# Second block's entry in three fp32r products with halves made on three engines, and 4 MB gate/up transfers for experts 18 to 29

## The reference, cut to what matters

```python
h = rmsnorm(x, g_attn_norm)
proj = h @ w_in                     # [256, 1024] @ [1024, 928]: 512 columns u, 256 q_lat, 128 kv_lat, 32 k_r
y_pool = pool_mixer(u, w_pool, b_pool, pool_scale)
y_attn = mla_attention(q_lat, kv_lat, k_r, cos, sin, g_q_a, w_q_b, g_kv_a, w_kv_b)
mix = concatenate([rmsnorm(y_pool, g_out_pool), rmsnorm(y_attn, g_out_attn)])
x = x + mix @ w_out
x = x + moe(rmsnorm(x, g_ffn_norm), ...)   # 32 experts, top 4 per token
return rmsnorm(x, g_final)
```

## Time and profile before

| | us |
|---|---|
| median of 3 runs | 1413.59 |
| range of the runs | 1408.78 to 1415.08 |
| profiled execution, its own time | 1410.57 |
| span of that execution | 1408.8 |

### The profile page before, as it was taken

The page is one execution under the profiler, slowest core; times in us unless marked ns, Lnnn a source line. Parts: engine busy times, 40 slices in busy tenths (PEclk is TensorE's granted clock), DMA queues, the critical chain, the costliest instruction groups (busy, mean ns, idle before and its releaser), DMA issues.

```text
span 1408.8 us, 21679 instructions
## 1 busy us (share of the span) xinstructions
PE 1360.4 (97%) x7688; PEld 775.7 (55%) x7689; DVE 755.0 (54%) x1157; ACT 304.4 (22%) x461; POOL 725.6 (52%) x727
## 2 busy tenths in 40 slices
PE   8999999999999999999999999999989999999997
PEld 7899989999967744334334334334333343334332
DVE  7575788887675545445356535444354453433322
ACT  5645453334325201001001001001000010001001
POOL 3000023332154078888878988888888888500000
PEclk9999999999999999999999999999999999999999
DMA  9444355555448899999999999999999999999996
GB/s 322 156 147 148 120 180 180 179 179 179 170 178 287 342 378 429 428 428 428 427 408 425 428 428 428 428 428 428 428 428 427 429 428 428 428 428 428 428 424 266
DMA packets 78283, 480.81 MB, mean 341 GB/s; under 512 B 7115, under 2 KB 31368, under 8 KB 53160
## 3 DMA queue, kind: packets, MB, share of 16 engines
q1 hardware_dynamic: 74910, 477.71, 83.5%
q10 hardware_dynamic: 3338, 2.62, 0.6%
HBM read 479.26 MB, written 1.05 MB: 341 GB/s over the span
## 4 chain that ended last, share of the span: by engine, by line
PE 55%; DMA 22%; issue 15%; POOL 5%; DVE 2%; ACT 0%; POOLq 0%; SPq 0%; DVEq 0%; ACTq 0%
DMA stage<-in_w_gate_up 14%; PE bank L2480 13%; DMA stage<-in_w_down 8%; PE bank L2158 7%; PE bank L1928 6%; PE bank L2588 6%; PE bank L2186 4%; POOL ring_b L677 3%; POOL ring L677 2%; PE bank L1878 2%; PE bank L2085 2%; PE bank L2123 2%; PE bank L1944 2%; PE bank L2466 1%; PE bank L2530 1%
## 5 line engine op out<-in xcount | busy, mean ns | idle before, releaser
L2480 PE MATMUL bank<-ring,x_T 128*64 128x512 f32 x1552 | 349.2, 596 | 22.1 <-POOL ring L677 16.2
L677 POOL COPY ring_b<-stage 128x1024 f32<-128x1024 f32 x252 | 264.9, 1097 | 47.1 <-DMA stage<-in_w_down 23.5
L2480 PEld LDWEIGHTS bank<-ring,x_T 128*64 128x64 f32 x1552 | 106.4, 137 | 244.1 <-issue 195.3
L2588 PE MATMUL bank<-ring_b,act_T 128*64 128x512 f32 x1056 | 233.9, 595 | 0.5 <-ACT act_T L1022 0.5
L677 POOL COPY ring<-stage 128x1024 f32<-128x1024 f32 x192 | 198.2, 1078 | 35.3 <-DMA stage<-in_w_gate_up 26.7
L1735 DVE TENSOR_TENSOR h<-h,bank 128x512 f32<-128x512 f32 x124 | 79.7, 684 | 190.8 <-PE bank L2530 190.8
L2588 PEld LDWEIGHTS bank<-ring_b,act_T 128*64 128x64 f32 x1056 | 72.9, 137 | 144.3 <-issue 129.4
L1711 DVE SCALAR_TENSOR_TENSOR y_lo<-bank,slot_gate,y_hi 128x512 fp32r<-128x512 f32 x33 | 24.8, 751 | 207.4 <-ACT y_hi L1002 207.4
L533 POOL TENSOR_TENSOR rstd<-msq,neg_half 128x2 f32<-128x2 f32 (+2 forms) x9 | 7.7, 856 | 240.7 <-DVE msq L1089 221.2
L574 POOL TENSOR_TENSOR ff_lo<-ring,ff_hi 128x2048 fp32r<-128x2048 f32 x11 | 53.0, 4818 | 145.2 <-PE bank L2158 96.6
L1016 ACT ACTIVATE sig<-bias_raw 128x512 f32<-128x512 f32 x33 | 20.8, 629 | 489.4 <-DVE bias_raw L1746 489.4
(11 more groups left out here) (491 smaller groups left out, 2124.4 us busy)
## 6 DMA issues: line engine op xcount, KB each, us to landing
stage<-in_w_gate_up SPq DMA_DIRECT2D x73, 2048.0 KB, 15.1
stage<-in_w_down SPq DMA_DIRECT2D x38, 2048.0 KB, 15.2
stage_b<-in_w_gate_up SPq DMA_DIRECT2D x25, 2048.0 KB, 15.0
ring<-in_w_gate_up SPq DMA_DIRECT2D x21, 2048.0 KB, 23.8
ring_b<-in_w_down SPq DMA_DIRECT2D x13, 2048.0 KB, 23.0
stage_b<-in_w_down SPq DMA_DIRECT2D x12, 2048.0 KB, 15.2
ring<-in_w_in SPq DMA_DIRECT2D x22, 1024.0 KB, 5.2
ring<-in_w_ffn_in SPq DMA_DIRECT2D x22, 1024.0 KB, 6.2
```

The lines of the kernel that those rows point to most:

```text
L677: ins = pool.tensor_copy(pair_slot(g, k)[:, cols], stage_place(g, place)[:, cols])
L2480: ins = pe.matmul(banks[n][rows, :], t.x_T[:, c, :], job_slot(g, c)[:, c0:c0 + 512], start=False, stop=(c == GU - 1), skip_group_check=True)
L2588: ins = pe.matmul(banks[4][rows, :], t.act_T[:, k, SLOTS * (c // 2):SLOTS * (c // 2) + SLOTS], job_slot(g, GU + c)[:, c0:c0 + 512], start= ...
```

## The change

1. *Entry in three products.* ACT rounds the four chunks of w_in_2 (`entry_rounded`, order 0, 3, 1, 2; high parts in free places of `ff_hi` and in a new `w_u_hi`) and the four quarters of the normalised rows (`rows_rounded`). The rests are spread: DVE chunk 0, half of chunk 3 and half of chunk 2, POOL chunk 1 and the other halves (`entry_rest`), and POOL the four quarters of `h_n_lo`. SP issues chunk 3 ahead of chunk 2. PE's `lat0`, `lat1`, `u1`, `u0` take three fp32r products each in a new order.
2. *Squares.* The squares of `x_n` go from DVE to ACT (`gained_square`).
3. *Constants.* POOL's constants for the routing move from the start of the entry to behind the pooling windows.
4. *Gate/up in quads.* `STAGED = E - 14`: experts 2 to 17 are staged. For experts 18 to 29 SP loads gate/up as two transfers of 4 MB (`load_quad`, rows of 32 KB), each when TensorE has used both pairs; POOL waits for each quad and passes it on to the two pairs' semaphores. Expert 30 is loaded in parts of 2 MB, expert 31 in halves as before. So that a quad is contiguous in SBUF, pairs 0 and 1 lie in `ring`, pairs 2 and 3 in `ring_b`; SP's early loads of parts 2 and 3 of expert 0 are swapped with it.
5. *Row order.* A partition now holds four neighbouring rows of w_gate_up, so ACT writes `h_n` permuted and the gathers read 128 contiguous columns.

The diff, cut to its core:

```diff
-STAGED = E - 6
+STAGED = E - 14
+STAGED_USES = 16 * (PLACES + (STAGED - 2) * PARTS) // PLACES
...
+ENTRY = 4
+ENTRY_ORDER = (0, 3, 1, 2)
+def entry_made(c):
+    return ENTRY_ORDER.index(c) + 1
...
 # sync_program
+    def load_quad(e, quad):
+        sp.dma_start(quad_slot(g, quad), gate_up[e, quad]).then_inc(s.staged[0] if quad else s.quad_in, 16)
...
-    for n, (src, shape, _) in enumerate(g.second):
+    for n in (0, 1, 3, 2, *range(4, len(g.second))):
+        src, shape, _ = g.second[n]
...
-    with sp.Fori(STAGED - 1, E - 2) as m:
+    with sp.Fori(STAGED - 1, E - 3) as m:
         last = last_job(m)
-        for k in range(PARTS):
+        for quad in range(2):
+            sp.wait_ge(*part_used(g, last, 2 * quad + 1))
+            load_quad(m + 1, quad)
+        for k in range(PAIRS, PARTS):
             next_part(m + 1, last, k)
...
 # gpsimd_program
+    def entry_rest(c, half=None):
+        slot, cols = slot_use(g.n_second + c)[0], entry_cols(c, half)
+        pool.wait_ge(s.pa_rounded, entry_made(c))
+        pool.tensor_tensor(t.ring_r[:, slot, cols], t.ring[:, slot, cols], entry_high(g, c)[:, cols].bitcast(F32),
+                           ALU.subtract).then_inc(s.pa_split, 1)
+    entry_rest(1)
+    entry_rest(3, 1)
+    for n, (b, h) in enumerate((b, h) for b in range(NB) for h in range(2)):
+        rows, toks = slice(4 * h, 4 * h + 4), slice(b * P, b * P + P)
+        pool.wait_ge(s.h_rounded, 2 * NB + n + 1)
+        pool.tensor_tensor(t.h_n_lo[:, rows, toks], t.h_nT2[:, rows, toks], t.h_n_hi[:, rows, toks].bitcast(F32),
+                           ALU.subtract).then_inc(s.h_split_pool, 1)
     pool.wait_ge(s.ff_o, FF_STEPS)
...
     pool.tensor_tensor(mean, mean, r1, ALU.mult).then_inc(s.rstd_ready, 1)
+    entry_rest(2, 1)
     rsqrt("lat")
...
 # scalar_program
+    entry_rounded(0)
+    act.wait_ge(s.ff_g, FF_STEPS)
+    act.wait_ge(s.ff_o, FF_STEPS - 1)
+    for c in ENTRY_ORDER[1:]:
+        entry_rounded(c)
+    square("end1", s.rows_added, 2, 0, scratch)
+    rows_rounded(0, 0)
+    rows_rounded(0, 1)
+    act.wait_ge(s.act_msq, squares + 1)
+    square("end1", s.rows_added, 4, 1, scratch)
+    rows_rounded(1, 0)
+    act.wait_ge(s.act_msq, squares + 2)
+    gained_square(0)
+    rows_rounded(1, 1)
+    act.wait_ge(s.act_msq, squares + 3)
+    gained_square(1)
...
 # vector_program
+    entry_rest(0)
+    entry_rest(3, 0)
     dve.wait_ge(s.gains, 1)
     for b, n in ((0, 0), (0, 1), (1, 0)):
         add_rows(b, n)
     for h in range(2):
         turned_rows(0, h)
     add_rows(1, 1)
-    for h in range(2):
-        turned_rows(1, h)
+    turned_rows(1, 0)
     dve.wait_ge(s.small_in, 16 * 5)
-        dve.tensor_tensor(t.x_n[:, b, :], t.h[:, b, :], t.g_rows[:], ALU.mult).then_inc(s.h_gained, 1)
+    gained(0)
+    turned_rows(1, 1)
+    gained(1)
+    entry_rest(2, 0)
+    dve.wait_ge(s.act_msq, ACT_SQUARES["end1"])
...
 # tensor_program
+    LATENT = ((t.h_n_hi, wl_hi), (t.h_n_hi, wl_lo), (t.h_n_lo, wl_hi))
+            if k % 4 == 0 and part == 0:
+                pe.wait_ge(s.h_rounded, 2 * NB + 2 * b + k // 4 + 1)
+                pe.wait_ge(s.pa_rounded, entry_made(k // 4))
+            if k % 4 == 0 and part == 1:
+                pe.wait_ge(*((s.pa_split, 1) if k else (s.w_split, SPLIT + 1)))
+            if k % 4 == 0 and part == 2:
+                pe.wait_ge(s.h_split_pool, 2 + 2 * b + k // 4 + 1)
+    first = open_bank(r2, "lat0")
+    latents(first, 0, 0)
+    pe.wait_ge(s.rows_added, 2 * NB)
+    turn_quarter(r2, "nT", t.h, 1, 1)
+    latents(first, 0, 1)
+    other = open_bank(r2, "lat1")
+    for k0 in (0, 4):
+        for part in range(2):
+            latents(other, 1, part, k0, k0 + 4)
+    latents(first, 0, 2).then_inc(s.filled, 1)
+    latents(other, 1, 2).then_inc(s.filled, 1)
...
-            k_rows = slice(2 * P * (f // 2) + f % 2, 2 * P * (f // 2) + 2 * P, 2)
+            k_rows = slice(P * f, P * f + P)
```

More of the change, by code:

```diff
@@ L255, in build @@
         t.persistent(into(ctx))
[L257 removed]
+        for phase in (t.vectors, t.mixer, t.branches, t.ffn, t.attention, t.entry, t.last_out, t.experts):
             with ExitStack() as stack:
@@ L688, in gpsimd_program @@
                 put_in_place(last, k, place, m * 48 + 16 * landed)
+    with pool.Fori(0, E - 2 - STAGED) as m:
+        for quad in range(2):
+            pool.wait_ge(*((s.staged[0], m * 16 + (STAGED_USES + 16)) if quad else (s.quad_in, m * 16 + 16)))
+            pool.sem_inc(s.turn_begun, 1)
+            for pair in (2 * quad, 2 * quad + 1):
+                pool.sem_inc(s.in_place[pair], 16)
     rsqrt("end2")
@@ L913, in scalar_program, with entry_rounded, rows_rounded, gained_square @@
     act.preload_act_table_set("natural_log_exp_and_others")
-    for b in range(NB):
-        square("end1", s.rows_added, 2 * b + 2, b, t.y_att[:].rearrange("p b n -> p (b n)"))
-        if b == 0:
-            act.wait_ge(s.act_msq, ACT_SQUARES["end1"] - 1)
+    def entry_rounded(c):
+        slot, value = slot_use(g.n_second + c)
+        act.wait_ge(s.landed[slot], value)
+        act.activation(entry_high(g, c)[:, entry_cols(c)], t.ring[:, slot, entry_cols(c)],
+                       ACT.Copy).then_inc(s.pa_rounded, 1)
+    def rows_rounded(b, h):
+        rows, toks = slice(4 * h, 4 * h + 4), slice(b * P, b * P + P)
+        act.wait_ge(*r2.drained(f"nT{b}{h}"))
+        act.activation(t.h_n_hi[:, rows, toks], t.h_nT2[:, rows, toks], ACT.Copy).then_inc(s.h_rounded, 1)
+    def gained_square(b):
+        act.wait_ge(s.h_gained, b + 1)
+        act.activation(scratch, t.x_n[:, b, :], ACT.Square,
+                       accum_out=t.msq[:, NORM_AT["end1"], NB + b:NB + b + 1]).then_inc(s.act_msq, 1)
+    scratch = t.y_attn[:].rearrange("p b n -> p (b n)")
+    squares = ACT_SQUARES["end1"] - 2 * NB
+    entry_rounded(0)
[14 more added lines that the diff above has]
+    gained_square(1)
     act.wait_ge(s.rstd_ready, NORM_AT["attn"] + 1)
@@ L1442, in turned_rows, with entry_rest, gained @@
                           spread(t.gain2[:, 4 * h:4 * h + 4], P), ALU.mult).then_inc(done, 1)
+    def entry_rest(c, half=None):
+        slot, cols = slot_use(g.n_second + c)[0], entry_cols(c, half)
+        dve.wait_ge(s.pa_rounded, entry_made(c))
+        dve.tensor_tensor(t.ring_r[:, slot, cols], t.ring[:, slot, cols], entry_high(g, c)[:, cols].bitcast(F32),
+                          ALU.subtract).then_inc(s.w_split, 1)
+    def gained(b):
+        dve.wait_ge(s.rows_added, 2 * b + 2)
+        dve.tensor_tensor(t.x_n[:, b, :], t.h[:, b, :], t.g_rows[:], ALU.mult).then_inc(s.h_gained, 1)
+    k = NORM_AT["end1"]
+    entry_rest(0)
+    entry_rest(3, 0)
     dve.wait_ge(s.gains, 1)
@@ L2235, in tensor_program, with entry_parts, entry_weights @@
-    landed(n + 2)
-    landed(n + 3)
-    wu = halves(n + 2, 512)
-    def u_block(bank, i, j, k0=0, k1=KT):
+    def entry_parts(c):
+        slot, cols = slot_use(n + c)[0], entry_cols(c)
+        return [w[:, cols].rearrange("p (k m) -> p k m", k=4) for w in (entry_high(g, c), t.ring_r[:, slot, :])]
+    def entry_weights(c0):
+        parts = [entry_parts(c) for c in (c0, c0 + 1)]
+        return [[parts[k // 4][i][:, k % 4, :] for k in range(KT)] for i in range(2)]
+    wl_hi, wl_lo = entry_weights(0)
@@ new lines, in tensor_program, with latents @@
+    LATENT = ((t.h_n_hi, wl_hi), (t.h_n_hi, wl_lo), (t.h_n_lo, wl_hi))
+    def latents(bank, b, part, k0=0, k1=KT):
+        x, wt = LATENT[part]
+        for k in range(k0, k1):
+            if k % 4 == 0 and part == 0:
[5 more added lines that the diff above has]
+                pe.wait_ge(s.h_split_pool, 2 + 2 * b + k // 4 + 1)
+            ins = pe.matmul(bank[:, 0:416], x[:, k, b * P:(b + 1) * P], wt[k][:, 0:416],
+                            start=(part == 0 and k == 0), stop=(part == 2 and k == KT - 1))
+        return ins
@@ L2245, in u_block @@
         return ins
     into = open_bank(r2, "u1")
-    u_block(into, 1, 0)
+    for part in range(2):
+        u_block(into, 1, 0, part)
     pe.wait_ge(s.diag_ready, NB)
@@ L2253, in tensor_program @@
     ins.then_inc(s.filled, 1)
-    u_block(into, 1, 1, 0, 6)
+    for part in range(2):
+        u_block(into, 1, 1, part)
+    u_block(into, 1, 0, 2)
+    u_block(into, 1, 1, 2, 0, 4)
     pe.wait_ge(s.lat_ready, 2 * NB)
@@ L2278, in tensor_program @@
     into = open_bank(r2, "u0")
-    u_block(into, 0, 0)
-    u_block(into, 0, 1).then_inc(s.filled, 1)
+    for j in range(2):
+        for part in range(3):
+            ins = u_block(into, 0, j, part)
+    ins.then_inc(s.filled, 1)
     def bias(m, o):
```

127 lines of the change are left out of this document (71 added, 56 removed).

## The result

The changed kernel takes 1417.89 us (median of 8 executions, 1416.34 to 1424.68), the kernel before 1410.2 in executions taken beside it (8, 1408.78 to 1415.08). The ratio is 1.0056, with a 95% interval of 1.0041 to 1.0072: slower by 7.7 us. The profiled execution took 1416.46 us, its span is 1414.5 against 1408.8.

A forecast was written before the change was run, and what follows sets the result against it. The last 900 us were taken as bound by expert weight transfers, whose start hangs on TensorE's entry. Entry +7.4, gathers -0.6 and -1.2, transfers -2.4 sum to +3.2 us: 1416.8 for the median, range 1408 to 1422.5.

The forecast's parts named there:

- Products of the entry: Entry on TensorE: three fp32r products per step save 4.2 us if all halves are ready, bounds 3.5 and 4.9.
- Chunk 3 and DVE: Entry: DVE waits for chunk 3, first add_rows at 394.0, TensorE stands from 389.7 to 394.9, latents start at 398.2.
- DVE and POOL hold each other up: Entry: SBUF work of both engines stands in one line, 10.9 us, making rsqrt("end1") 7.5 us late, at 409.2.
- Behind it: Entry after rsqrt("end1"): latents' transposes start 8.9 us late, heads' transposes 7.4 us late.
- Constants: POOL's constants moved behind the pooling cost nothing; without idle time to cover them, up to 6 us.
- Gathers: Contiguous gather columns: -0.6 us ahead of the stream, -1.2 us at the expert with two jobs.
- Transfers: Gate/up of experts 18 to 29 in 32 KB rows: -2.4 us from fewer packets, bounds 0 and -4.8.
- The rival from the Trainium skill: Transfers: 2 MB already gives full bandwidth, so 32 KB packets bring nothing; 1419.2 us, chance 10%.
- Direct loading: From expert 18 on: zero cost, up to +1 us; TensorE's 4.9 us later start is caught up within the job.
- the second: Rival: clock falls to half in TensorE's entry gap if over about 4 us; 1419.8 to 1422.2 us, chance 20%.
- DVE and POOL don't queue: Rival on the entry: the engines alternate with little loss; entry +2 to +3, total 1412 us, chance 17%.
- does what it says: Rival: chunk 3 is there in time and the 4.2 us saving arrives whole; 1405.2 us, chance 8%.

The follow-up runs named there:

- e9: Changed kernel with entry reordered: ACT rounds all rows before chunks 3 and 2, DVE and POOL take their rests of chunk 3 later; 1420.28 us, ratio 1.0064.
- e1: Changed kernel with the expert part of before (POOL copies up to expert 25, no 4 MB transfers), keeping new entry and contiguous gathers; 1419.79 us, ratio 1.0061.
- e7: Changed kernel with 16 idle products on TensorE ahead of its wait for the first row transposes; 1418.71 us, ratio 1.0045.
- e12: Changed kernel with five idle TensorE products ahead of the third pair of slots, in jobs from the nineteenth on; 1419.66 us, ratio 1.0072.
- e5: Changed kernel with DVE's half rest of chunk 3 moved from ahead of the add_rows to behind turned_rows(1, 0); 1419.82 us, ratio 1.0058.
- e6: Changed kernel with DVE's late rest of chunk 3, ACT rounding 0, 1, rows, 3, 2, and POOL's half of chunk 3 later; 1414.16 us, ratio 1.0025.
- e8: Changed kernel without POOL's four h_n_lo subtractions, products reading h_n_hi instead, so the rows' rests are missing from results; 1413.92 us, ratio 1.0027.
- e3: Changed kernel with 4 MB transfers for experts 18 to 27 only, 28 and 29 in 2 MB transfers; 1415.95 us, ratio 1.0041.
- e2: Changed kernel with direct loading from expert 18 on, but in 2 MB transfers (rows of 16 KB); 1418.97 us, ratio 1.0059.
- e10: Kernel before with the change's expert part, 4 MB transfers for experts 18 to 27 only, and the old entry; 1407.44 us, ratio 0.9986.
- e4: Kernel before with the whole expert part (4 MB transfers for experts 18 to 29, contiguous gathers) and the old entry; 1409.73 us, ratio 1.0000.
- e11: Changed kernel with the reordered entry of e9 and 4 MB transfers for experts 18 to 27 only; 1413.84 us, ratio 1.0024.

## Why the prediction was right, and where it was not

**The time.** 1416.8 was forecast, 1417.89 came, inside the range. Two errors cancelled, and that the forecast lies within 1.1 us is luck. The three executions shown of before have a median of 1413.59, over eight it is 1410.2: the base was 3.4 us too high. And the medians differ by 7.7 us, not 3.2: 4.5 too little. The forecast gave 0.68 to a time that can't be told from no change and 0.22 to slower; beside the kernel before, the interval of 1.0041 to 1.0072 says slower. Between the two profiled executions the change costs 5.9 us (5.7 in the spans); the other 1.8 of the medians' difference is where these two stand among their own (0.1 and 1.8 us above the lowest). Of the 2.5 between 3.2 and 5.7, the tail is 2.0.

**Products of the entry.** Right in kind, but it bought nothing. Sixteen steps of 128x416 fp32r products now take 9.7 us of TensorE where nothing holds them (e9, 392.2 to 401.9, transposes included), against 11.6 for the sixteen fp32 steps (0.70 each, and the same 0.36 of transposes). The saving is there, but up to `diag` TensorE is no longer what sets the time.

**Chunk 3 and DVE.** Right: first `add_rows` at 394.13 (forecast 394.0), gap 5.40 (5.2), latents 399.52 (398.2; with half the time at 1.2 GHz, in e1, e7 and e12, they start at 398.9 to 399.1, so the clock accounts for most of the 1.3). e5 and e6 show what the forecast said in one breath: DVE and ACT both wait, and only freeing both pays, 3.7 us.

**DVE and POOL hold each other up.** Right: 10.9 us in line, rsqrt at 409.2, measured 409.06. e8 gives it a price of 3.0 (2.6 against e3's profile of the same entry). This step rested on one pair of rows, and that pair decided between 1412 and 1416.8.

**Behind it.** qlT's transposes +8.1 (8.9), heads' transposes +6.9 (7.4). Right.

**Constants.** Zero, as said: POOL still stands idle for 4.45 us before `rsqrt("pool")`.

**Gathers.** -0.3 before the stream (-0.6): the two gathers take 3.76 and 2.00 us where they took 3.95 and 2.10. -1.1 at the expert with two jobs (-1.2).

**Transfers.** -2.1 us where -2.4 was forecast, and a packet's fixed part of 12 ns as worked out from the earlier trace rows (192 of them are 2.3 us, not 2.4). The rate of 432 to 433 GB/s that was to show it did not come; from 990 to 1340 us it is 430. The rival from the Trainium skill ("DMA: Bandwidth & Descriptors", Rules for kernel authors), that 1 MiB per DMA is enough, would have given 0; 430 against 428 GB/s is small, but it is there, and e2 has it gone. With the tail that they lengthen, the quads pay nothing: from 380 MB left to the end 908.4 us in the changed kernel, 908.7 in e2, and only cut short by two experts 905.7 (e3).

**Direct loading.** The step that failed: "at most 28 us of the 29.4", "caught up within the job". I took a job's work from a busy share over 400 us. It is 26.2 us for most jobs, and 30.3 for one; that one is expert 29, the last to be loaded in quads. A mean hid the only job without slack, at the place with the least time left to catch up. +2.0 us instead of 0, shown by e3 and e10, where the tail is 16.9 and 17.3 us, and not cured by a full clock (e12). The means of the eight profiles with these quads and the six without differ by 2.0 too (19.6 and 17.6).

**Rivals.** The clock did fall in the gap, as the second said. Its sum of +6.2 to +8.6 takes in the 7.7 between the medians, but not for its reason: it had the entry at +10.4, which is +6.9. Its price of 3 us was wrong: that price assumed that TensorE is the path, while POOL's line was. Nor does its limit of about 4 us of standstill hold, taken from one stretch of idle time: at the quads the clock fell behind pauses of 2 us. "DVE and POOL don't queue" fell by e8, "does what it says" by the first rows.

**Open.** Why executions of the new entry show falls of the clock behind the gap more often than those of the old one (between 414 and 510 us: eight of eleven profiles, none of the three of before, e4 and e10) was not run down. What they go with can be read from the profiles: the way from the heads' transposes to 380 MB left takes 71.7 to 72.0 us in the six without a fall between 440 and 510 us, 72.6 to 72.7 in the four with one of 3.4 us (e1, e5, e8, e12), 77.0 with 13.6 us (e7, e9) and 77.7 with 17.1 us (e6, e11). So they are worth up to 6 us, and more than one of the medians above contains them. No edit took them away, so that the clock is the cause is argued.
